# Gathering the tokens' rows once per group of eight experts, and picking each pair's rows with a 0/1 matrix

## What is computed

```python
grp = argmax(h @ w_group + b_group)                 # one group of 4 per token
le = (h @ w_router + b_router) of that group        # 8 logits
top_p, top_i = lax.top_k(softmax(le), 2)            # two experts of that group
gate = p_grp * top_p / sum(top_p)
expert = grp * 8 + top_i
a = silu(x_rows @ w_gate[e]) * (x_rows @ w_up[e])   # 2048 x 768 each
y = a @ w_down[e]                                   # 768 x 2048
out = rmsnorm(x + sum of gate * y over the token's two experts)
```

## Time and profile before

| | us |
|---|---|
| median of 3 runs | 1971.58 (1970.26 to 1972.33) |
| the profiled execution's own time | 1971.26 |
| its span, first to last instruction | 1969.5 |
| mean granted TensorE clock, share of full | 0.971 |
| PE busy | 1836.4 (93%) |
| DMA, mean over the span | 347 GB/s |
| data moved by DMA | 684.02 MB |

### The profile page before, as it was taken

How to read it: one execution, slowest core, us unless ns; L and a number is a source line. 1 busy time by engine, 2 the same in 40 slices (tenths; PEclk the granted TensorE clock), 3 DMA queues, 4 the chain that set the end, 5 groups by cost and what they waited for, 6 DMA issues and landing times.

```text
span 1969.5 us, 21061 instructions
## 1 busy us (share of the span) xinstructions
PE 1836.4 (93%) x9334; PEld 1033.4 (52%) x9334; DVE 602.9 (31%) x834; ACT 182.5 (9%) x292; POOL 260.6 (13%) x107
## 2 busy tenths in 40 slices
PE   8999999999999999889898989889898999889896
PEld 7878888888744444344343444434343444434442
DVE  6212838611231332222231222222222322222224
ACT  4000101111201000000100000000000000000003
POOL 6434544433200000000000000000000000000001
PEclk9999999999999999999999999999999999998998
DMA  9232224344789999999999999999999999999996
GB/s 359 82 102 86 87 90 137 143 176 145 265 341 427 423 430 431 430 431 430 431 430 430 431 429 430 431 430 430 431 429 431 430 431 431 428 432 430 430 429 273
DMA packets 68456, 684.02 MB, mean 347 GB/s; under 512 B 10676, under 2 KB 11316, under 8 KB 41016
## 3 DMA queue, kind: packets, MB, share of 16 engines
q1 hardware_dynamic: 65528, 674.84, 82.4%
q0 software_dynamic: 2304, 8.39, 1.1%
q10 hardware_dynamic: 576, 0.14, 0.0%
HBM read 683.35 MB, written 8.39 MB: 351 GB/s over the span
## 4 chain that ended last, share of the span: by engine, by line
PE 66%; DMA 32%; DVE 1%; issue 0%; ACT 0%; SPq 0%; DVEq 0%; ACTq 0%
PE banks L1283 20%; DMA region_h<-in_w_gate 16%; DMA region_h<-in_w_up 15%; PE banks L910 13%; PE banks L1303 11%; PE banks L1081 9%; PE banks L1218 4%; PE banks L906 2%; PE banks L1203 2%; DMA region_rest<-in_w_down 1%; PE banks L1192 1%; PE banks L939 1%; PE banks L1294 1%; DVE region_w L1803 0%; PE banks L1116 0%
## 5 line engine op out<-in xcount | busy, mean ns | idle before, releaser
L1283 PE MATMUL banks<-region_rest,region_w 128*64 128x384 f32 x2048 | 348.7, 494 | 35.4 <-DMA region_rest<-in_w_gate 34.6
L1777 DVE TENSOR_TENSOR region_x<-banks,region_x 128x1024 f32<-128x1024 f32 x120 | 141.4, 1220 | 579.5 <-PE banks L1218 579.5
L1303 PE MATMUL banks<-region_rest,region_w 128*64 128x512 f32 x1080 | 276.6, 669 | 27.5 <-DVE region_w L1803 19.3
L1283 PEld LDWEIGHTS banks<-region_rest,region_w 128*64 128x64 f32 x2048 | 144.4, 138 | 234.6 <-issue 167.3
L564 POOL TENSOR_TENSOR split_w<-region_rest,split_w 128x2048 fp32r<-128x2048 f32 x42 | 197.8, 4710 | 267.6 <-DVE split_w L1441 267.4
L910 PE MATMUL banks<-split_h,split_w 128*128 128x512 f32 x736 | 230.2, 392 | 0.0
L1283 PE MATMUL banks<-region_h,region_w 128*64 128x384 f32 x1024 | 173.7, 492 | 44.2 <-DMA region_h<-in_w_gate 24.4
L1303 PEld LDWEIGHTS banks<-region_rest,region_w 128*64 128x64 f32 x1080 | 83.6, 154 | 201.0 <-issue 173.1
L625 POOL DMA_INDIRECT region_h<-x_rows,region_rest x16 | 16.1, 1006 | 1247.9 <-PE banks L1203 1206.7
L1283 PE MATMUL banks<-region_w 128*64 128x384 f32 x1024 | 172.1, 489 | 0.4 <-DMA region_w<-in_w_up 0.4
L1081 PE MATMUL banks<-split_w,split_h 128*128 128x512 f32 x512 | 159.2, 392 | 0.0
(11 more groups left out here) (249 smaller groups left out, 1256.7 us busy)
## 6 DMA issues: line engine op xcount, KB each, us to landing
region_rest<-in_w_down SPq DMA_DIRECT2D x45, 3072.0 KB, 28.8
region_rest<-in_w_gate SPq DMA_DIRECT2D x32, 3072.0 KB, 23.6
region_rest<-in_w_up SPq DMA_DIRECT2D x30, 3072.0 KB, 23.9
region_w<-in_w_up SPq DMA_DIRECT2D x17, 3072.0 KB, 30.7
region_h<-in_w_gate SPq DMA_DIRECT2D x16, 3072.0 KB, 23.7
region_h<-in_w_up SPq DMA_DIRECT2D x15, 3072.0 KB, 22.3
region_h<-in_w_down SPq DMA_DIRECT2D x15, 3072.0 KB, 24.0
region_w<-in_w_gate SPq DMA_DIRECT2D x14, 3072.0 KB, 32.2
```

Of the source, the lines that this page charges most:

```text
L1283: mm = t_.matmul(ps[h * SLOTS:(h + 1) * SLOTS, u, 0:HF], hTe[:, k, :], ring_gu[slot][:, kk, h * HF:(h + 1) * HF], start=(k == 0), stop=(k ...
L1303: mm = t_.matmul(ps[g * SLOTS:(g + 1) * SLOTS, 6 + n, :], aT[:, kk, q * SLOTS:(q + 1) * SLOTS], ring_down[slot][:, kk, (2 * c + n) * 512:( ...
L1777: v.tensor_tensor(tile, ps[:, 2 + 2 * c:4 + 2 * c, :], tile, ALU.add).then_inc(comb_added, 1)
```

## The change

For pair 0 all stays: its rows are gathered with the plan's list and turned by transposes. From pair 1 on:

- `gather_group` gathers the first 128 tokens of a group of eight experts (four pairs) into `hg`, at i = 1, 4, 8 and 12. Each token has a rank in its group, counted on PE (`of_token` in `count_experts`) and turned into numbers by six small DVE steps. `plan_group` (PE) and `read_rows` (DVE) make the list `gidx[1]`.
- `gather_extra` runs for each pair from 1 on: POOL clears `hx` (128 partitions of 8 KB) and gathers into it those rows of the pair whose rank is 128 or more. All other entries of its list are out of bounds. It waits for the group's gather to have landed.
- `choose_rows` takes the place of `transpose_rows` for pairs 1 to 15: for each of 16 column blocks one float32 product of `hg` (128 x 128, the stationary operand) with the 0/1 matrix `chosen` (128 x 64) and one of `hx` (64 x 128) with the identity, added in PSUM.
- `chosen` is made by DVE as its transpose (`compare_rows`), turned on PE (`turn_choice`) and copied by DVE (`read_rows`). `turn_choice` and `plan_group` stand on PE between the two down tiles of b = 0 (for pair 1, after the first tile of expert 1).
- The first gate row block of expert 1 is loaded on its own into `early_row`, as soon as pair 0's rows have landed. The pieces of that tile shift by one row block.
- `keep_clock_half`, a product of 256 columns that nobody reads, is added at two places of the routing part.
- `id_cmp` and `zero32` move to other places.

```diff
+GROUP_PAIRS = EG // 2
...
+        hx = at(W0 + 20 * KB, D)
+        chosen = at(W1 + 31 * KB + NA * 8, P)
+        group_key = at(W1 + 31 * KB + NA * 8 + P, NT)
+        group_rank = at(W1 + 31 * KB + NA * 8 + P + NT, NT)
+        row_rank = at(W1 + 31 * KB + NA * 8 + P + 2 * NT, 1)
+        row_near = at(W1 + 31 * KB + NA * 8 + P + 2 * NT + 1, 1)
+        chosen_T = at(W1 + 28 * KB, P)
+        early_row = at(W0 + 25 * KB, 2 * HF)
...
+            sp.wait_ge(rows_gathered, 16)
+            sp.dma_start(early_row, wg_v[1, :, 0, :]).then_inc(row_landed, 16)
+            for n, at_row in ((RING + 1, 1), (RING + 2, 0)):
                 expert, part = nth_tile(n)
                 src, q = (wg_v, wu_v)[part // 2], part % 2
+                middle = q * QK + at_row + QK // 2
                 sp.wait_ge(half_used, n - RING)
-                sp.dma_start(ring_gu[slot_of(n)][:, first_half, :], src[expert, :, q * QK:q * QK + QK // 2, :])\
+                sp.dma_start(ring_gu[slot_of(n)][:, 0:QK // 2, :], src[expert, :, q * QK + at_row:middle, :])\
                     .then_inc(half_landed, 16)
                 sp.wait_ge(tile_used, n - RING)
-                sp.dma_start(ring_gu[slot_of(n)][:, second_half, :], src[expert, :, q * QK + QK // 2:(q + 1) * QK, :])\
+                sp.dma_start(ring_gu[slot_of(n)][:, QK // 2:QK - at_row, :], src[expert, :, middle:(q + 1) * QK, :])\
...
+            def gather_group(i):
+                pool.wait_ge(group_read, i)
+                g.indirect_dma_start(out=hg, out_offset=None, in_=x2_dram,
+                                     in_offset=bass.IndirectOffsetOnAxis(ap=gidx[1], axis=0),
+                                     bounds_check=T - 1, oob_is_err=False)\
+                    .then_inc(group_gathered, 16)
+
+            def gather_extra(i):
+                g.memset(hx, 0.0).then_inc(extra_cleared, 1)
+                pool.wait_ge(extra_cleared, i)
+                pool.wait_ge(plan_read, i * 9 + 1)
+                pool.wait_ge(group_gathered, 16 * (i // GROUP_PAIRS + 1))
+                g.indirect_dma_start(out=hx, out_offset=None, in_=x2_dram,
+                                     in_offset=bass.IndirectOffsetOnAxis(ap=gidx[0], axis=0),
+                                     bounds_check=T - 1, oob_is_err=False)\
+                    .then_inc(extra_gathered, 16)
+
+            for i in range(1, PAIRS):
+                if i == 1:
+                    pool.wait_ge(tile_used, PARTS + 1)
+                pool.wait_ge(hte_ps, i * 4)
+                pool.sem_inc(turns, 1)
+                if i == 1 or i % GROUP_PAIRS == 0:
+                    gather_group(i)
+                gather_extra(i)
             n_over = pool.value_load(over_i[0:1, OVER:OVER + 1], min_val=0, max_val=OVER)
 
...
+            def keep_clock_half():
+                t_.matmul(ps[:, 4, 0:256], ident, x_sb[:, 0, 0:256], start=True, stop=True)
 
...
             keep_clock(RANK_FILL)
+            keep_clock_half()
...
+            def choose_rows(i, b):
+                pe.wait_ge(chosen_ready, i)
+                pe.wait_ge(extra_gathered, i * 16)
+                pe.sem_inc(turns, 1)
+                r = slice(b * SLOTS, (b + 1) * SLOTS)
+                of_group = hg.rearrange("p (c k) -> p k c", k=KT)
+                extra_k = hx[r, :].rearrange("p (c k) -> p k c", k=KT)
+                for k in range(KT):
+                    out_k = ps[:, 2 + k // 8, (k % 8) * SLOTS:(k % 8 + 1) * SLOTS]
+                    t_.matmul(out_k, of_group[:, k, :], chosen[:, r], start=True, stop=False)
+                    mm = t_.matmul(out_k, extra_k[:, k, :], ident[r, r], start=False, stop=True)
+                    if k % 8 == 7:
+                        mm.then_inc(hte_ps, 1)
+
+            def turn_choice(i):
+                pe.wait_ge(chosen_T_ready, i)
+                t_.transpose(ps[:, 5, P:2 * P], chosen_T, ident).then_inc(chosen_ps, 1)
+
+            def plan_group(i):
+                pe.wait_ge(group_pick, i)
+                for t in range(NT):
+                    mm = t_.matmul(ps[:, 4, 500:502], pick[:, t, :], asg_split[:, t, 0, 0:2], start=(t == 0), stop=(t == NT - 1))
+                mm.then_inc(group_ps, 1)
 
...
+                    row = early_row if kk < early else ring_gu[slot][:, kk - early, :]
                     for h in (0, 1):
                         mm = t_.matmul(ps[h * SLOTS:(h + 1) * SLOTS, u, 0:HF], hTe[:, k, :],
-                                       ring_gu[slot][:, kk, h * HF:(h + 1) * HF],
+                                       row[:, h * HF:(h + 1) * HF],
...
+                of_token = ohg.rearrange("p a b -> p (a b)")
+                t_.matmul(ps[:, 6, 256:256 + NT * G], before, of_token, start=True, stop=False)
+                for n in range(1, NT):
+                    mm = t_.matmul(ps[:, 6, 256 + n * G:256 + NT * G], ones, of_token[:, 0:(NT - n) * G],
+                                   start=False, stop=(n == NT - 1))
+                mm.then_inc(group_counted, 1)
...
             keep_clock(GATHER_FILL - 1)
+            keep_clock_half()
...
+                    if b and not part:
+                        pe.wait_ge(row_landed, 16)
+                    gate_up(part, landed_first(PARTS * b + part), halves=(not b and part < 2), early=int(b and not part))
+                    if b and not part:
+                        turn_choice(1)
+                        plan_group(1)
                 if b:
-                    transpose_rows(1, 0)
+                    choose_rows(1, 0)
                     transpose_act(b)
                     pe.wait_ge(m_lo_ready, 2)
                 else:
...
                         plan(i + 1)
-                        transpose_rows(i, 1)
+                        choose_rows(i, 1)
                     else:
-                        transpose_rows(i + 1, 0)
+                        choose_rows(i + 1, 0)
                     transpose_act(i * 2 + b)
                     pe.wait_ge(at_ready, i * 2 + (b + 1))
                     pe.wait_ge(m_lo_ready, i * 4 + 2 * b)
                     for part in (4, 5):
                         down(b, part, landed(i, PARTS * b + part))
+                        if not b and part == 4:
+                            turn_choice(i + 1)
+                            plan_group(i + 1)
 
             gates_up(PAIRS - 1, 0, 0)
-            transpose_rows(PAIRS - 1, 1)
+            choose_rows(PAIRS - 1, 1)
             transpose_act(E - 2)
...
+                if ranked:
+                    then(v.tensor_scalar(row_rank, ps[:, 5, 6:7], -1.0, None, ALU.add))
+                    then(v.tensor_scalar(row_near, row_rank, float(P), float(2 * T), ALU.is_lt, ALU.mult))
+                    v.scalar_tensor_tensor(gidx[0], ps[:, 5, 0:1], float(NOBODY), row_near, ALU.add, ALU.add).then_inc(plan_read, 1)
+                else:
+                    v.tensor_scalar(gidx[0], ps[:, 5, 0:1], float(NOBODY), None, ALU.add).then_inc(plan_read, 1)
...
+            def compare_rows(i):
+                v.tensor_scalar(chosen_T, row_slot[0], row_rank, None, ALU.is_equal).then_inc(chosen_T_ready, 1)
+                if i % GROUP_PAIRS == 0:
+                    then(v.tensor_scalar(group_key, group_key, -float(T), None, ALU.add))
+                v.tensor_tensor(pick[:, 0:NT], row_slot[0].rearrange("p (a b) -> p a b", a=1).to_broadcast([P, NT, P]),
+                                group_key.rearrange("p (a b) -> p a b", b=1).to_broadcast([P, NT, P]),
+                                ALU.is_equal).then_inc(group_pick, 1)
+
+            def read_rows(i):
+                ve.wait_ge(chosen_ps, i)
+                v.tensor_copy(chosen, ps[:, 5, P:2 * P]).then_inc(chosen_ready, 1)
+                ve.wait_ge(group_ps, i)
+                v.tensor_scalar(gidx[1], ps[:, 4, 500:501], float(NOBODY), None, ALU.add).then_inc(group_read, 1)
+
...
+            ve.wait_ge(group_counted, 1)
+            then(v.tensor_tensor(r4, ps[:, 6, 256:256 + NT * G].rearrange("p (t g) -> p t g", t=NT), ohg, ALU.mult))
+            then(v.tensor_reduce(group_rank, r4, AX.X, ALU.add))
+            then(v.scalar_tensor_tensor(group_key, v4[:, 1, :], -float(T), group_rank, ALU.mult, ALU.add))
+            then(v.tensor_scalar(group_key, group_key, float(G * T), None, ALU.add))
+            each = group_rank.rearrange("p (a b c) -> p a b c", b=1, c=1).to_broadcast([P, NT, 2, 2])
+            then(v.tensor_scalar(asg_split[:, :, :, 6:8], each, 1.0, None, ALU.add))
...
                     if not b and 0 < i < PAIRS - 1:
-                        read_plan(i + 1, 1 - s)
...
+                    if not b and 0 < i < PAIRS - 1:
+                        compare_rows(i + 1)
+                        read_rows(i + 1)
                     if e < E - 2:
                         store_rows_T(e + 1)
                     if e == 0:
-                        read_plan(1, 1)
+                        read_plan(1, 1, True)
```

35 lines of the change are left out of this document (19 added, 16 removed).

## The result

The changed kernel takes **2455.19 us** (median of five runs, 2453.81 to 2457.14), the kernel before 1971.58 beside it (1970.26 to 1972.70). The ratio is 1.2456, with a 95% interval from 1.2442 to 1.2471. Beside the later runs the kernel before was executed 25 times: 24 of them lie between 1968.4 and 1972.7, and one slow execution, 3068.27 us at a granted clock of 0.553, is left out of the ratios. The forecast was 2030, range 2000 to 2105: the side is right, the size is not. The rest of this document is about where the other 425 us are.

What follows compares the result with a forecast made beforehand. PE, no longer the loads (88.3 us a pair), was to bound at 78.5 + 10.8 + 0.6 = 89.9, with clock 90.5; 650.5 + 14 x 90.5 + 110.2 + 1.8 gives 2029.5, said as 2030 us, range 2000 to 2105.

Steps and rivals of the forecast that it cites:

- a record of the new products: In choose_rows on PE: 0.112 us a record, 64 records in 7.3 us, twice a pair.
- My upper bound of 0.119: Highest price in us for a record in choose_rows, from the old transposes' total of 1.90 us for 16 records.
- the upper bounds: Whole kernel with PE at 90.8 us a pair and the clock's loss at up to 4: named as 2065 us.
- 0.6 us for a pair: Loss on PE from clock falls around the small products between up and down tiles, range 0 to 4 us.
- a fall in every stretch: Rival: the clock falls in every choose_rows, 6 us a pair more than 89.9, time 2105; chance 0.20.
- The wait at pair 1: PE waits 11.4 us for two late gathers before choose_rows; rows at 622.4, pair 1 begins at 650.5, not 623.9.
- The gathers at i = 4, 8 and 12: Two gathers and list take 34.1 us against PE's 37.6: hidden, with 3.5 us to spare.
- Waits for tiles: Sign in the profile: PE's waits for weight tiles are gone after pair 1.
- DVE costs PE nothing: DVE's added small steps are covered by PE's work: nothing; without cover PE would wait about 2 us a pair.
- The side of the forecast: Whole kernel: slower than before, 3.0%; chances slower 0.89, within 4 us 0.04, faster 0.07.
- Loads still pace, and the stall costs them what was won: Rival: a record under 0.10 us, 9.0 us won, 8 to 12 lost at pair 1, no change; chance 0.05.
- The faster rival: Loads pace, records under 0.10 us and choose_rows(1, 0) waits less than 3 us: 1963 us; chance 0.07.

Runs made afterwards that it cites:

- run 7: The changed kernel with hg and hx read in contiguous blocks (permuted columns, another output) and the product of hx over all 128 partitions: 2096.02 us.
- run 5: The changed kernel with the product of hx taken over all 128 partitions instead of 64, same result: 2298.97 us.
- run 4: The kernel before with its 16 transposes written as float32 products, same operands and same step of 16: 2074.31 us.
- run 9: The changed kernel with choose_rows reduced to the 16 transposes of hg; gathers, plans and waits stay: 1977.64 us.
- run 10: As run 9, but pair 1 gathered as in the kernel before and the group's gather first at pair 2: 1966.24 us, ratio 0.9980.

## Why the prediction failed in size

**The step that failed** is the one that prices a record of the new products: "The nearest row is count_experts ... 0.112 us for a record ... The weight load of 128 columns sets the step in both". The row was read rightly, and run 7 returns it to the digit. But it was not the nearest in what matters. Its stationary operand is `ones`, read without a step, and always 128 high. The new operands have a step of 16, which doubles the record at full clock (0.218 in run 5), and two heights in turn, which make it 0.29, and 0.31 at half clock. I compared the height and the number of columns and not how the columns are read. My upper bound of 0.119 came from the transposes, which do have the step, and that made the step look free. A transpose's price says nothing of a product's: run 4 changes nothing else and the record goes from 0.119 to 0.223. (No run times a contiguous transpose, so what the step costs a transpose isn't measured.)

In the sum: 2 x (19.7 - 7.3) = 24.8 us of the 29.0 by which the mean pair went over its forecast (119.5 for 90.5). Times 14, with another 12.4 in the last pair and 6.3 at the wait, that is 366 of the 426 us. A part of it is the clock's: at full clock all through, 0.288 a record would make 18.4 us of the 19.7.

One figure of the forecast was also added up wrongly: 90.8 us of PE and 4 of clock are 94.8 a pair and make 2090, not the 2065 named for the upper bounds. The stated range ends at 2105 either way.

**The clock** is the second term. I took 0.6 us for a pair and gave a fall in every stretch as a rival, at 5 to 6. It did fall in every stretch: 5.3 in pair 1 on the activations and down tiles, 4.7 more than I took, or 66 us in 14 pairs (with the 366 that is 6 too many, as pair 1 by its parts is 0.5 longer than the mean pair). My chance of 0.20 was too low, and my reason against it ("the new products stream more") didn't hold: PE was busy without a gap all through the new products and the clock fell in them (0.59 in the stretch of run 5, 0.50 in that of the changed kernel). In run 7, where the record costs what I had put in, a mean pair takes 95.1 us, for 95.9 in this rival and 90.5 in my forecast, and the time is 2096.02 for 2105 and 2030. So even with the record I had assumed I would have been 66 too low, by the clock. That the rival's sum came so near is partly luck: it had 3 us for a fall in each half, and run 7 has one fall in a pair that costs 6.1.

**What held.** The wait at pair 1: rows at 622.4 forecast, the first product at 622.98; issue at 594.7 for 596.2, landings of 15.0 and 12.3 us for 13.8 and 12.4. PE waited 13.6 instead of 11.4: it was there 1.6 earlier, by what the fillers won in pair 0, and the rows came 0.6 later. Pair 1 begins at 656.88 for 650.5, which is the dearer products (19.9 for 13.6) and little else. The gathers at i = 4, 8 and 12 are hidden: L1261 waited 13.6 us in all. Waits for tiles are gone, and q0 moved 4.91 MB. DVE costs PE nothing: 0.7 us of idle time before L1353 in the whole span.

**The side of the forecast** rested on less than it seemed. It held because the products were dear. But run 9, which has none of them, is still 6.6 to 8.5 us above before by the stall, as I had it in the rival "Loads still pace, and the stall costs them what was won" (1970 to 1974, at most 3 above before, measured 1977.64). The faster rival needed the wait to be small; run 10 removes it and is 4.8 faster, not 9.

**Two rules beside the rows.** The Trainium skill, "TensorE: Matmul & The Clock Gate", section "LDWEIGHTS (loading the stationary operand)", says that a weight load's time follows its columns alone, whatever the height. With one height the runs agree (0.218 at 128 partitions, 0.223 at 64); with two in turn they don't (0.29 to 0.31). The Trainium skill, "SBUF — State Buffer", section "Specifications (TRN2)", says that SBUF is read in lines of 16 bytes and wants two hits in each for full bandwidth. By that a step of 16 float32, 64 bytes, puts every element into a line of its own. The products' rows fit it at full clock, 0.218 against 0.112, but not at half, 0.217 against 0.213; that the lines are the reason isn't shown. The transposes had the same step at 0.119.

## What to carry over

Before you price a product from another row of the same trace, compare four things: form (a transpose is no product), type, the step with which its stationary operand is read, and the height of its neighbours. In a stream of small float32 products keep the stationary operand contiguous and all heights equal, even if half of what is multiplied is zeros, and look at the clock in the stretch before you credit either. Where loads bound a kernel, look at what the first iterations wait for: of 16.9 us by which run 9 began pair 1 later, 12.2 stood at pair 15, and the room in later pairs gave nothing back.
